# Value pages of the paged cache laid with two tokens on a partition and two pages above each other, in a one-core decoder layer

## The reference, cut to what matters

```
k_past = cache_k[layer, pages].reshape(past_len, A_HEADS, A_HEAD_DIM)
v_past = cache_v[layer, pages].reshape(past_len, A_HEADS, A_HEAD_DIM)
...
p = jax.nn.softmax(logits, axis=-1)      # over the blocks selected and the own block
...
out = jnp.einsum('hqnk,hqnkd->hqd', p_sel, v_sel) + jnp.einsum('hqk,hkd->hqd', p_own, v_own)
```

## Time and profile before

| what | value |
|---|---|
| median of 3 runs | 1300.35 us (1300.03 to 1301.06) |
| the profiled execution's own time | 1299.43 us |
| its span, first to last instruction | 1297.4 us |
| mean granted TensorE clock | 0.979 of 2.4 GHz |
| TensorE busy with matmuls | 1165.5 us, 90% of the span |
| DMA over the span | 368.15 MB, mean 284 GB/s |

### The profile page before, as it was taken

How to read it: one execution, slowest core, us unless ns; L and a number is a source line. 1 busy time by engine, 2 the same in 40 slices (tenths; PEclk the granted TensorE clock), 3 DMA queues, 4 the chain that set the end, 5 groups by cost and what they waited for, 6 DMA issues and landing times.

```text
span 1297.4 us, 20453 instructions
## 1 busy us (share of the span) xinstructions
PE 1165.5 (90%) x7849; PEld 735.6 (57%) x7849; DVE 524.7 (40%) x1094; ACT 225.0 (17%) x506; POOL 230.4 (18%) x279
## 2 busy tenths in 40 slices
PE   3999998999999989999999997999978788778796
PEld 2344443465667658888888455656544354444463
DVE  3398966524253554454454447221211111111112
ACT  4122225431222321201100222000000000000000
POOL 2432344200010411430000101111111101111001
PEclk9999999999999999999999996999999989999999
DMA  9997999998253434215433727999999999999994
GB/s 354 372 283 280 356 378 386 378 379 323 70 166 104 126 106 115 57 38 139 122 130 130 267 63 235 420 415 417 411 420 420 417 416 419 417 414 418 415 414 167
DMA packets 118392, 368.15 MB, mean 284 GB/s; under 512 B 12604, under 2 KB 58573, under 8 KB 98966
## 3 DMA queue, kind: packets, MB, share of 16 engines
q1 hardware_dynamic: 93408, 304.44, 60.5%
q0 software_dynamic: 21328, 55.24, 13.8%
q10 hardware_dynamic: 3558, 7.13, 1.8%
HBM read 354.61 MB, written 22.36 MB: 291 GB/s over the span
## 4 chain that ended last, share of the span: by engine, by line
PE 65%; DMA 23%; SPq 4%; DVE 3%; issue 2%; ACT 2%; DVEq 0%; ACTq 0%; POOLq 0%
PE ps L1941 62%; DMA hx<-in_w_exp_gate 10%; DMA ring<-in_w_exp_gate 6%; DMA ring<-in_w_exp_up 4%; PE ps L1952 3%; SPq L583 2%; SPq L588 1%; DMA ring<-in_cache_v 1%; DMA work<-in_x_prompt 1%; DMA ring<-in_cache_k 1%; DMA h_rows<-ring 1%; DVE work L1560 0%; SPq L554 0%; DVE work L1896 0%; SPq L556 0%
## 5 line engine op out<-in xcount | busy, mean ns | idle before, releaser
L1941 PE MATMUL ps<-ring,work 128*64 128x256 f32 (+4 forms) x2064 | 295.5, 438 | 42.0 <-DMA ring<-in_w_exp_up 16.6
L1941 PEld LDWEIGHTS ps<-ring,work 128*64 128x64 f32 (+2 forms) x2064 | 157.9, 139 | 161.6 <-issue 84.0
L1941 PE MATMUL ps<-hx,ring 128*128 128x272 f32 x928 | 218.2, 397 | 7.6 <-DVE work L1560 7.6
L1941 PE MATMUL ps<-ring,hx 128*32 128x256 f32 (+3 forms) x1232 | 209.3, 458 | 7.1 <-ACT hx L879 3.6
L1941 PEld LDWEIGHTS ps<-hx,ring 128*128 128x128 f32 x928 | 177.7, 192 | 45.8 <-issue 6.6
L1941 PEld LDWEIGHTS ps<-ring,hx 128*32 128x32 f32 (+1 forms) x1232 | 108.1, 139 | 94.3 <-issue 75.7
L1941 PE MATMUL ps<-work 128*32 128x256 f32 (+12 forms) x1186 | 134.0, 398 | 21.0 <-DVE work L1255 10.0
L1941 PE MATMUL ps<-hx,work 128*64 128x256 f32 (+2 forms) x784 | 114.3, 412 | 22.0 <-DMA hx<-in_w_exp_up 9.2
L1894 DVE TENSOR_TENSOR work<-work,ps 128x256 f32<-128x256 f32 x32 | 13.5, 421 | 251.1 <-ACT work L1200 251.1
L800 POOL DMA_INDIRECT out<-work x32 | 50.5, 1578 | 328.5 <-DVE work L1906 328.5
L1941 PEld LDWEIGHTS ps<-hx,work 128*64 128x64 f32 (+2 forms) x784 | 69.5, 144 | 66.9 <-issue 29.5
(11 more groups left out here) (333 smaller groups left out, 932.4 us busy)
## 6 DMA issues: line engine op xcount, KB each, us to landing
ring<-in_w_exp_gate SPq DMA_DIRECT2D x21, 2048.0 KB, 40.8
ring<-in_w_exp_down SPq DMA_DIRECT2D x42, 1024.0 KB, 39.2
ring<-in_w_exp_up SPq DMA_DIRECT2D x21, 2048.0 KB, 40.7
ring<-in_w_ada SPq DMA_DIRECT2D x12, 2048.0 KB, 17.4
hx<-in_w_exp_gate SPq DMA_DIRECT2D x11, 2048.0 KB, 41.1
hx<-in_w_exp_up SPq DMA_DIRECT2D x10, 2048.0 KB, 39.3
work<-in_w_exp_down SPq DMA_DIRECT2D x20, 1024.0 KB, 39.3
ring<-in_cache_v SPq DMA_DIRECT2D x64, 256.0 KB, 9.7
```

Source lines behind the costliest of these rows:

```text
L1941: return pe.matmul(out, lhsT, rhs, start=start, stop=stop, **k)
```

## The change

A value page is laid over 64 partitions with two tokens (4 KB) on each. The four pages 2i of a unit (q = 0 to 3) lie on partitions 0 to 63, the four pages 2i + 1 (q = 4 to 7) on partitions 64 to 127, in the same columns. Key pages stay as they are. The rows on the partitions of a unit are then the tokens 256 i + 2 t + u for partition t and u = 0 or 1, so the softmax weights are transposed from every second column of a stretch of 256, and a product takes its columns at another place of the unit. The numbers of DMAs, transposes and matmuls stay the same: 128 value DMAs of 256 KB, 32 transposes, 8 matmuls per unit.

```diff
@@ load_pages
-                src = cache[0, bass.DynSlice(page, 1)].rearrange("a t h d -> (a t) (h d)")
-                eng.dma_start(slot(n)[:, AW * q:AW * q + AW], src).then_inc(sems[SLOT_ORDER[n]], 16)
+                if what == "k":
+                    src = cache[0, bass.DynSlice(page, 1)].rearrange("a t h d -> (a t) (h d)")
+                    dst = slot(n)[:, AW * q:AW * q + AW]
+                else:
+                    src = cache[0, bass.DynSlice(page, 1)].rearrange("a (t u) h d -> (a t) (u h d)", u=2)
+                    dst = slot(n)[64 * (q // 4):64 * (q // 4) + 64, 2 * AW * (q % 4):2 * AW * (q % 4) + 2 * AW]
+                eng.dma_start(dst, src).then_inc(sems[SLOT_ORDER[n]], 16)
@@ tensor
+            def page_pair(g, page):
+                return logits[g][:, 0:PAST].rearrange("p (i t u) -> p i u t", i=PAGES // 2, u=2)[:, page // 2, page % 2, :]
+
@@ weights_turned
-                            last = turn(ps[:, (6, 1)[q % 2], P * (page % 4):P * (page % 4) + P], logits[0][:, P * page:P * page + P])
+                            last = turn(ps[:, (6, 1)[q % 2], P * (page % 4):P * (page % 4) + P], page_pair(0, page))
@@ later_weights_turned
-                        last = turn(ps[:, 1, P * (page % 4):P * (page % 4) + P], logits[1][:, P * page:P * page + P])
+                        last = turn(ps[:, 1, P * (page % 4):P * (page % 4) + P], page_pair(1, page))
@@ page_values
-                        q = 4 * (page % 2) + j
+                        q = 2 * j + page % 2
```

## The result

The changed kernel takes 1367.53 us, the median of 4 runs (1367.15 to 1373.74), against 1300.70 us for the kernel before (4 runs, 1300.03 to 1303.19). The ratio is 1.052 (95% interval 1.050 to 1.054): 67 us slower. The forecast was 1338 us in a range of 1300 to 1366; the direction and the place were right, and the range was left by 1.5 us.

The account below looks back on a forecast made before the run. The value stage was taken as bound by the full DMA stream, with TensorE's loop nearly equal. 36.1 (stream) + 0.5 (transposes) + 1 (clock) = 37.6 us on 1299.43 gave 1337, or 1338 us against the runs' median; range 1300 to 1366.

Parts of the forecast that it names:

- What bounds the stage: Value-page stage, 162 to 249 us: DMA stream full at 383 GB/s, TensorE's loop nearly equal, slack 4.4 us.
- Larger packets: SyncE's half of the value stream gets 4 KB packets: 1.5 us less stream, at most 3.5 us back on the path.
- Half the partitions: Value DMAs writing 64 partitions: 262 GB/s, doubled from near's 131 with 16 partitions; + 36.1 us.
- The lower bound from the earlier trace: Value stream no slower than 222 GB/s, from x_sample's load to 32 partitions; + 59.1 us.
- The rival that is nearest to the measured time: Value stream: narrow entry worse than taken, 218 to 222 GB/s, + 59.1 + 1.5, 1361 us; chance 0.10 for below 222.
- the likeliest case: Value stream: both queues in one half at 222 to 290 GB/s, 1338 us, range + 21 to + 60; chance 0.50.
- Both queues in one half: SyncE and GpSimd walk a unit's pages in the same order, so both write the same 64 partitions most of the time.
- opposite halves half of the time: Rival for the value stream: 311 GB/s, harmonic mean of 262 and 383, + 17, 1317 us; chance 0.20 for 290 to 370.
- The sum: Last value unit's arrival: 161.9 + 128.1 + 2 = 292.0 us at 262 GB/s, against use at 255.87; + 36.1 us.
- Transposes: The 32 weight transposes reading every second column cost 0.5 us in all, bounds 0.5 to 3.2.
- The clock: TensorE's clock falls after waits for pages; paid only behind the last value unit, 1 us, bounds 0 and 4.

Follow-up runs that it names:

- the two with the whole computation: Changed kernel with value pages on every second partition and weights reordered to match, for all units or only v0 to v11: 1300.67 and 1301.12 us.
- the fast layout: Changed kernel with each value page on every second partition in place of a contiguous half, softmax weights not rearranged: 1298.38 us, ratio 0.998.

## Why the prediction was right in kind and short in size

**What bounds the stage: right.** Two nearly equal bounds were read from the earlier trace rows, "a faster stream can give back little; a slower one is felt at once". The slower stream is felt nearly whole, 65.0 us at v15, and the faster ones gave nothing (the two with the whole computation have intervals that hold 1) or, with mismatched weights, 0.25%. The shift is passed on unreduced to the end, as read from the earlier trace rows.

**Larger packets: right.** SyncE's packets doubled, its lag vanished where the entries allowed it (6.4 us to landing), and the rate of the fast layout in the middle of the stage, 408 GB/s, lies between the prediction's two sizes: 1.5 us less for the stream, which is 390 GB/s, and 420. It was right too that this saves next to nothing: of the 3.5 us that it set as the most that can come back, the trace of the fast layout shows 0.5 at v15.

**Half the partitions: the step that failed, in size.** "I take a doubling from 16 to 64, 262 GB/s." The rate is 218. What failed is the scaling from near's loads to these: from 131 GB/s the growth is a factor of 1.66 and not 2, and it is over at 32 partitions (221). Why it is short of 2 stays open. Near's rate is itself 120 to 136 in kernels that load it in the same way, and twice the lowest of these would still be 240. The lower bound from the earlier trace rows, 222 GB/s, was close to the right value, and I had set it aside for the start latency inside its 0.7 us. That it was so close is in part luck. The DMA view of that window, from 713.5 to 714.2 us of the kernel before, counts 0.16 MB:

```profile
DMA packets 50, 0.16 MB, mean 222 GB/s; under 512 B 12, under 2 KB 12, under 8 KB 50
```

x_sample has 0.13 MB, so the row holds the first packets of x_prompt too, and x_sample alone gives at most 187 GB/s over these 0.7 us. The figure of the Trainium skill (SBUF — State Buffer, Door 1: The DMA port swizzle), about 218 GB/s for partitions 0 to 63, is what the windows show. The prediction's sum at 218 GB/s gives 61.9 + 1.5 = 63.4 us and so 1364, not the 1362 that stands there. The rival that is nearest to the measured time, 1361 us, had a chance of only 0.10. One end of the likeliest case is off as well: 290 GB/s gives + 25 us by the same sum, and not + 21.

**Both queues in one half: right, shown twice.** Giving each queue a half, or turning GpSimd's order round, brings 312 GB/s. But the rival "opposite halves half of the time" reckoned with 383 GB/s for the time in which they are apart. Apart all the time they give 312, and with that the harmonic mean with 262 would have been 285 and not 311. The Trainium skill (SBUF — State Buffer, Can I just issue two DMAs to hit both halves?) gives two concurrent DMAs on the two halves as 6% faster than one; with the two full queues of this kernel the gain was 312 against 218 GB/s, 43%. The two cases are not quite the same, since 218 is already the rate of two queues, but for full queues the trace disagrees, and the measurement decides.

**The sum.** 33.55 MB at 218 GB/s are 153.9 us, and 161.1 + 153.9 + 2 = 317.0 us; v15 started at 320.9. So the formula itself was 3.9 us short. It counted value pages alone, and other bytes pass in the same stretch. The DMA view from 161 to 319 us, so up to 2 us before the last use:

```profile
DMA packets 10974, 35.12 MB, mean 222 GB/s; under 512 B 2091, under 2 KB 2202, under 8 KB 10960
```

So 1.6 MB that are not value pages passed with them: the end of the key pages, part of an output of 1 MB from ScalarE's queue, and the first w_in pieces, issued from 287.65 us. At 218 GB/s they are 7.2 us; a part of that is won back, since the mean over the stretch is 222. The order of size is that of the 3.9 us.

**Transposes: right.** 8 in 1.23 us against 1.09 or 1.14 is 0.018 or 0.011 us each, 0.4 to 0.6 us for all 32, 0.5 taken; by themselves they move the time by nothing that can be measured.

**The clock: short by 1.3 us.** 1 us was taken, 2.3 were lost between v15 and the first w_in product, inside the bounds of 0 and 4. The windows of the stage show a granted clock of 0.83 over 148 us, a mixture of 2.4 and 1.2 GHz; while pages bind (the DMA share stays at 1.04), this is hidden, and it is paid only behind the last unit.

**What would have come nearer.** With 222 GB/s from the earlier trace rows the prediction's own term is 59.1 us, and with the rest of its sum 60.6. Measured, 218 in place of 222 adds 153.9 - 151.1 = 2.8 us, the start at 161.1 takes off 0.8, and the remainder of 3.9 found above closes it: 65.0 us, v15's shift. With 2.3 us behind v15 that is 67.3 of the 68.0 us of span; 0.7 us are not accounted for.

## What to carry to other kernels

Ask of every layout change which partitions one DMA writes, and which partitions the other DMAs in flight write at that moment. In this kernel 64 neighbouring partitions at a time took a full stream from 383 to 218 GB/s, two queues in opposite halves reached 312, and every second partition of 128 kept the full rate. When a stream and an engine are nearly equal bounds, a change to the stream has much to lose and little to win. And of two rows that bound an unmeasured rate, weigh the one with the form nearest to the new transfer more than the one from which a scaling must be told; look also at what else lies in a short window, and at how far the same row moves from one run to the next.

## What the runs showed of the hardware that was not expected

- DMA engines show a share of 1.04 while they move 218 GB/s, and 1.03 at 408: a full share says that packets are under way, not that bytes flow. Time per MB on one queue, 4.83 us against 2.65, told the two apart.
- Halves used by separate queues at the same time gave 312 GB/s and not twice 218.
- SyncE's issue of a value page takes longer when it writes 64 partitions with 4 KB each: 477 ns against 338 before, in all 64 issues (medians). With every second partition it is 483, with 32 partitions of 8 KB 321. GpSimd's hardly changed (509 and 536 ns). The line of the page loads by its issues, in the changed kernel (ns min/median/max):

```profile
L561 SPq DMA_DIRECT2D ring<-in_cache_v x64: 477/477/687, 161.1 to 282.5; - x64
...
L561 POOL DMA_DIRECT2D ring<-in_cache_v x64: 509/509/724, 161.5 to 282.7; - x64
```

It costs nothing here (the kernel with every second partition has the same issues and is not slower), since SyncE waits for buffers; by an estimate from these numbers, on a queue that is bound by its issues, 64 of them would cost 64 x 139 ns = 8.9 us.
